# A two-layer diffusion step with linear attention: both passes of the linear attention re-ordered, its element-wise work spread differently over the engines

## The reference

```
z = h @ w_in                        # q, k (4 heads x 128), v, og (1024 each), r (2 x 16)
g = log_sigmoid(r @ gate_w + b)/16  # one decay per head, key column and direction
per chunk:  b = cumsum(g)
  o = (q*exp(b)) @ S + (sum over j<=i of q_i exp(b_i-b_j) k_j) v_j
  S = exp(b_last) * S + (k*exp(b_last-b))^T @ v
o = forward scan + backward scan
o = rms_norm per head(o, norm_g) * silu(og);   mix = o @ w_out
```

## Time and profile before

| | us |
|---|---|
| median of 3 runs | 2907.3 (2906.81 to 2907.7) |
| the profiled execution | 2904.5 |
| its span in the trace | 2902.7 |
| PE busy | 2770.3 (95%) |
| DVE busy | 1490.0 (51%) |
| ACT busy | 1267.4 (44%) |
| POOL busy | 159.4 (5%) |
| mean granted PE clock | 0.986 |

### The profile page before, as it was taken

The page is one execution under the profiler, slowest core; times in us unless marked ns, Lnnn a source line. Parts: engine busy times, 40 slices in busy tenths (PEclk is TensorE's granted clock), DMA queues, the critical chain, the costliest instruction groups (busy, mean ns, idle before and its releaser), DMA issues. The chain is left out here.

```text
span 2902.7 us, 39699 instructions
## 1 busy us (share of the span) xinstructions
PE 2770.3 (95%) x15219; PEld 2442.7 (84%) x15219; DVE 1490.0 (51%) x2282; ACT 1267.4 (44%) x2059; POOL 159.4 (5%) x260
## 2 busy tenths in 40 slices
PE   5999999999999999999999987778999999999998
PEld 3878887789999999999898876766899999999997
DVE  4255666655555445444413668775645554445444
ACT  5134445544444434333324765554543443334333
POOL 0000000000000000000000028810000000000000
PEclk9999999999999999999999998899999999999999
DMA  7643323533444444344214430024344344444443
GB/s 266 212 135 108 97 85 111 162 119 122 124 125 151 121 126 150 121 128 124 76 55 146 145 107 8 1 88 166 117 124 124 121 147 129 124 124 151 124 128 109
DMA packets 301702, 355.53 MB, mean 122 GB/s; under 512 B 22230, under 2 KB 244892, under 8 KB 300540
## 3 DMA queue, kind: packets, MB, share of 16 engines
q1 hardware_dynamic: 293840, 333.36, 37.0%
q10 hardware_dynamic: 5708, 12.42, 1.2%
q0 software_dynamic: 2016, 7.86, 0.8%
HBM read 338.27 MB, written 15.34 MB: 122 GB/s over the span
## 5 line engine op out<-in xcount | busy, mean ns | idle before, releaser
L1300 DVE TENSOR_TENSOR p_lo<-p_raw,p_hi 128x1024 fp32r<-128x1024 f32 x507 | 619.9, 1224 | 659.2 <-ACT p_hi L773 658.6
L773 ACT ACTIVATE p_hi<-p_raw 128x1024 fp32r<-128x1024 f32 x507 | 533.3, 1053 | 528.4 <-DMA p_raw<-mlp_w 413.1
L2087 PE MATMUL ps<-hm_hi,p_hi 128*128 128x384 f32 x1536 | 515.5, 336 | 0.8 <-DVE p_lo L1300 0.8
L2087 PE MATMUL ps<-hm_hi,p_lo 128*128 128x384 f32 x1536 | 515.8, 336 | 0.0
L2087 PE MATMUL ps<-hm_lo,p_hi 128*128 128x384 f32 x1536 | 514.4, 335 | 0.0
L2011 PE MATMUL ps<-p_hi,hid_hi 128*128 128x512 f32 x1152 | 362.6, 396 | 3.3 <-DVE p_lo L1300 3.3
L2011 PE MATMUL ps<-p_lo,hid_hi 128*128 128x512 f32 x1152 | 357.3, 391 | 0.0
L2011 PE MATMUL ps<-p_hi,hid_lo 128*128 128x512 f32 x1152 | 356.5, 391 | 0.0
L981 ACT ACTIVATE relu<-ps 128x384 f32<-128x384 f32 x192 | 94.5, 492 | 540.8 <-PE ps L2087 540.8
L1530 DVE TENSOR_TENSOR sqr<-relu 128x384 f32<-128x384 f32 x192 | 107.1, 558 | 390.7 <-ACT relu L981 390.7
L2087 PEld LDWEIGHTS ps<-hm_hi,p_hi 128*128 128x128 f32 x1536 | 288.4, 188 | 9.7 <-DVE p_lo L1300 2.5
(11 more groups left out here) (234 smaller groups left out, 3706.6 us busy)
## 6 DMA issues: line engine op xcount, KB each, us to landing
p_raw<-mlp_w SPq DMA_DIRECT2D x384, 512.0 KB, 3.9
mod_p<-mod_w SPq DMA_DIRECT2D x80, 512.0 KB, 4.1
p_raw<-gla_w_in SPq DMA_DIRECT2D x56, 512.0 KB, 3.6
p_raw<-gla_w_out SPq DMA_DIRECT2D x24, 512.0 KB, 3.3
mod_w<-mod_w SPq DMA_DIRECT2D x8, 1024.0 KB, 18.9
p_raw<-ab_w_in SPq DMA_DIRECT2D x14, 512.0 KB, 5.2
p_raw<-ab_w_out SPq DMA_DIRECT2D x24, 256.0 KB, 4.2
p_raw<-ab_w_out SPq DMA_DIRECT2D x12, 512.0 KB, 3.5
```

The costliest lines, as they stand in the source:

```text
L773: nc.scalar.activation(p_hi[s][:, :, 0:width], p_raw[s][:, :, 0:width], ACT.Copy).then_inc(pan_hi, 1)
L1300: V.tensor_tensor(p_lo[s][:, :, 0:width], p_raw[s][:, :, 0:width], p_hi[s][:, :, 0:width].bitcast(F32), ALU.subtract).then_inc(pan_lo, 1)
L2087: mm = M.matmul(ps[:, b, 0:GN], w[s][:, c, :], x[:, c, :], start=(c == 0 and x is hi and w is p_hi), stop=(c == DC - 1 and w is p_lo))
```

## The change

Five groups of edits, none of which changes what is computed.

1. The eight `turn_chunk`s of the projection stand in pairs behind its parts 3, 4, 5 and 6, no longer together behind part 7.
2. The last two groups of eight panels change places: og of group 2 comes before v of group 2, so the projection ends on `v_take`. ACT loads the exponential's table ahead of that `v_take` with an operation on one column. The loads of the masks and of the backward state go from ACT's queue to SP's. The two small exponentials `dec` move to tile 0's level index 3. PE no longer waits for all accumulators before the pass, POOL starts when all but two panels are used.
3. First pass: POOL does two operations a level with 512 columns each (at level 1: two with 256) into one of three buffers `gap` in place of four `dd`; ACT reads its half of a gap and writes in another order. `kh` is multiplied after level index 2. `state_step` stands after all levels, ahead of `q1`; `o_take` after level index 6; `att_out` does one head each after level indices 2 to 5.
4. Second pass: `from_state`, `update` and the state step run by pairs of heads. The gate is done by POOL in two operations of 1024 columns (times og, then times the reciprocal root, in place) in place of DVE's four of 256. `turn_o`, `gated_hi` and `gated_lo` run one to two tiles later.
5. The last two tiles are turned inside the output projection, after its panels 0 and 1. SP loads panel 2 after the last update and the others after the last `from_state`.

The diff, cut to its core:

```diff
+        def turned_after(part):
+            return (2 * part - 6, 2 * part - 5) if 3 <= part < 7 else ()
+        def value_panels(q):
+            return (q // DC % 2 == 0) != (q >= 4 * DC)
...
         def pool_gla(pool):
             pool.wait_ge(g_sum, 2 * GH)
-            pool.wait_ge(acc_done[GT - 1], ACC_AFTER_GLA_IN)
+            pool.wait_ge(pan_used, SLOTS + FEEDS_TO_GLA - 2)
...
-                if kind == "f" and n > 1:
-                    nc.gpsimd.tensor_tensor(x[:, :, 0, :], f_ref.broadcast_to(f[:, :, 0, :].shape), f[:, :, 0, :], ALU.subtract)
-                    nc.gpsimd.tensor_tensor(x[:, :, 1, :], b[:, :, 1, :], b_ref.broadcast_to(b[:, :, 1, :].shape),
-                                            ALU.subtract).then_inc(d_ready, 1)
+                x = out[:, :, :].rearrange("p u (b n) -> p b u n", n=n)
+                if n > 1:
+                    f_ref, b_ref = (y.unsqueeze(3).broadcast_to(f.shape) for y in (f_ref, b_ref))
+                    nc.gpsimd.tensor_tensor(x[:, :, 0::2], f, f_ref, ALU.subtract)
+                    nc.gpsimd.tensor_tensor(x[:, :, 1::2], b_ref, b, ALU.subtract).then_inc(d_ready, 1)
...
             pool_gla(pool)
+            pool.wait_ge(ob_taken, TILES)
+            for tile in range(TILES):
+                if tile:
+                    pool.wait_ge(o_sum, tile)
+                pool.wait_ge(og_in[tile % 2], 16 * (tile // 2 + 1))
+                if tile >= 2:
+                    pool.wait_ge(ot_ready, tile - 1)
+                nc.gpsimd.tensor_tensor(oo[tile % 2][:], o_b[tile][:], og[tile % 2][:], ALU.mult).then_inc(o_gate, 1)
+                pool.wait_ge(o_gate, tile + 1)
+                pool.wait_ge(o_rcp, tile + 1)
+                x = oo[tile % 2][:].rearrange("p (h v) -> p h v", h=GH)
+                nc.gpsimd.tensor_tensor(x, x, rs4[:, tile, 1, :].unsqueeze(2).broadcast_to([P, GH, DV]), ALU.mult).then_inc(o_nrm, 1)
... ACT, first pass
-                    nc.scalar.activation(out, dd[r % 4][:], ACT.Exp, scale=s).then_inc(e_ready, 1)
+                    x = gap_of(r)[:, 0::3, :] if kind == "S" else gap_of(r)[:, 1:3, :]
+                    y = out.rearrange("p h (b s n) -> p s (h b) n", s=2, n=n)
+                    nc.scalar.activation(y, x.rearrange("p s (b n) -> p s b n", n=n), ACT.Exp,
+                                         scale=-s if kind == "S" else s).then_inc(e_ready, 1)
... ACT, second pass
             for tile in range(TILES):
+                if tile >= 2:
+                    gated_hi(tile - 2)
                 head_norm(tile)
                 if tile + 2 < TILES - 1:
                     turn_take_k((2, 7)[tile % 2])
-                if tile:
-                    gated_hi(tile - 1)
-                    if tile + 1 < TILES:
-                        load_og(tile + 1)
+                if tile and tile + 1 < TILES:
+                    load_og(tile + 1)
...
                 if tile >= TILES - 2:
                     panel_hi()
... DVE, second pass
             for tile in range(TILES):
+                if tile >= 3:
+                    gated_lo(tile - 3)
...
                 if tile < TILES - 1:
-                    state_step(0, tile)
-                gate_head(tile)
+                    forward_step(tile, 0)
                 if tile:
-                    gated_lo(tile - 1)
+                    dve.wait_ge(o_ready, 2 * tile)
+                    V.tensor_tensor(o_b[tile][:], psf[:, 3 * 512:5 * 512], o_b[tile][:], ALU.add).then_inc(o_sum, 1)
+                    root_inverse(tile - 1)
+                if tile < TILES - 1:
+                    forward_step(tile, 1)
                 if tile >= TILES - 2:
                     panel_lo()
-            gated_lo(TILES - 1)
+            gated_lo(TILES - 3)
+            root_inverse(TILES - 1)
... PE, second pass
             for tile in range(TILES):
-                if tile:
-                    from_state(tile)
-                if tile < TILES - 1:
-                    update(TILES - 1 + tile, tile)
+                for pair in range(2):
+                    if tile:
+                        from_state(tile, pair)
+                    if tile < TILES - 1:
+                        forward_update(tile, pair)
                 if tile + 2 < TILES - 1:
                     turn_k0(tile + 2)
-                if tile:
-                    turn_o(tile - 1)
-            turn_o(TILES - 1)
-            pe.wait_ge(st_ready, 2 * (TILES - 1))
+                if tile >= 2:
+                    turn_o(tile - 2)
+            pe.wait_ge(st_ready, TILES - 1 + 2 * (TILES - 1))
+            pe.wait_ge(o_sum, TILES - 1)
... PE, output projection, behind each panel (ACT and DVE: gated_hi and gated_lo ahead of the panel's split)
+                    if layer and p < 2:
+                        turn_o(TILES - 2 + p)
```

More of the change, by code:

```diff
@@ L639, in factor_order @@
                         out += closing(TURNS[a - 1])
+                    if level == 2 and tile != 1:
+                        out.append(("k1", tile, 0))
                 if tile:
@@ L650, in gap_order @@
             for kind, tile, level in factor_order():
[L651 to L654, removed]
+                if kind == "M":
+                    out.append(("g", tile, level))
                 elif kind in ("k0", "q1"):
@@ L661, in gap_user, with gap_of, plain @@
         def gap_user(kind, tile, level):
-            if kind in ("k0", "q1"):
-                return factor_at[(kind, tile, level)]
-            return factor_at[("S" if kind == "f" and LEVELS[level] > 1 else "M", tile, level)]
+            return factor_at[("M" if kind == "g" else kind, tile, level)]
+        def gap_of(r):
+            return gap[r % len(gap)]
+        def plain(x):
+            return x[:, 0:2, :].rearrange("p u (h n) -> p (u h) n", n=P)
         def halves(t, level):
@@ L1519, in out_stage @@
                         pre_scale(layer, 0, 0)
+                    if layer and p < 2:
+                        gated_lo(TILES - 2 + p)
                     for k in turned_with(p):
@@ L2216, in update, with forward_update @@
                 for h in range(GH):
+                    last = M.matmul(psf[:, 5 * 512 + DV * h:5 * 512 + DV * (h + 1)], khn[n % 2][:, h, :],
+                                    gv[:, tile, DV * h:DV * (h + 1)], start=True, stop=True)
+                last.then_inc(upd_ready, 1)
+            def forward_update(tile, pair):
+                n = TILES - 1 + tile
+                if pair == 0:
+                    pe.wait_ge(khn_ready, n + 1)
+                pe.wait_ge(st_ready, n if tile == 0 else TILES - 1 + 2 * (tile - 1) + pair + 1)
+                for h in range(2 * pair, 2 * pair + 2):
                     last = M.matmul(psf[:, 5 * 512 + DV * h:5 * 512 + DV * (h + 1)], khn[n % 2][:, h, :],
@@ L2267, in _ @@
                             pe.wait_ge(ob_taken, a)
+                        else:
+                            for t in range(GT):
+                                pe.wait_ge(acc_read[t], acc_uses[t])
                         turn_k(kh, 3)
@@ L2278, in turn_k0, with from_state @@
                 turn_k(gk[:, tile], (2, 7)[tile % 2])
-            def from_state(tile):
+            def from_state(tile, pair):
                 pe.wait_ge(xt_ready, factor_at[("q0", tile, 0)] + 1)
```

164 lines of the change are left out of this document (92 added, 72 removed).

## The result

The kernel after takes 2854.9 us (median of 4 runs, 2853.3 to 2855.9) beside 2907.5 for the kernel before on the same chip: ratio 0.982, 95% interval 0.981 to 0.984. The forecast was 2869 with a range of 2853 to 2887. The profiled execution took 2855.85, its span 2854.1, so the spans differ by 48.6 us where the sum had 38.6. Most of the 13.8 us by which it came in under the forecast lie in the first pass. PE went from 2770.3 to 2752.2 us busy, DVE from 1490.0 to 1474.2, ACT stayed, and POOL went up by 21.

The account below looks back on a forecast made before the run. PE, busy 95% of the span, was taken as the bound, so only its waits could give much. Terms summing to -38.6 us took the profiled 2904.5 to 2865.9; with 2.8 for the median, 2868.7, told as 2869, range 2853 to 2887.

Parts of the forecast that it names:

- Edit 1 and the og group: Projection: transposes between parts gain 5.2 us; an og group in place of a v group loses 0.4.
- The turn: From projection to first pass: first gram at 1724.8 in place of 1729.92, a gain of 5.1 us.
- Tile 0: First tile of the first pass: a gain of 0.3 us for `kh` no longer at its head.
- The first pass: Eight tiles at 18.0 us in place of 20.17, bounded by DVE's 16.2 us of work: gain 17.4 us.
- the half-way step from 17.3 to the low-clock 18.6: First pass: a walked tile takes 17.3 us at full clock, 18.6 at low clock; 18.0 was taken.
- The second pass: First to last `from_state`: PE sets 4.9 and 4.45 us a tile, 1.6 for the start, 35.0 in all; gain 11.0.
- The tail: Last `from_state` to output panel 2: waits for ACT's and DVE's splits bind, 22.1 us against 22.3, gain 0.2.
- The offset: Whole kernel: the median of the runs lies 2.8 us above the profiled execution, added to the forecast.
- A: First pass keeps its pace, 20 us a tile, as several waits bind in turn: 2885 us; chance 0.15.
- B: Second pass becomes POOL's: 3.0 us per 1024-column operation, the gate sets 6.2 a tile: 2878 us; chance 0.08.
- C: First pass: POOL's four-index operation costs 2.1 us, not 1.1, a tile 28.6: slower, 2964 us; chance 0.05.
- D: The tail's waits don't bind and the low clock doesn't come: 2855 us; chance 0.10.

Follow-up runs that it names:

- Kernel 6: The kernel before with only the eight transposes moved, in pairs behind parts 3 to 6 of the projection: 2901.5 us.
- kernel 7: The kernel after with v before og at the projection's end, as before the change: 5.93 us from last panel to first gram of a level, 3.02 in the kernel after.
- Kernel 1: The kernel after with the multiplication of `kh` at the head of the tile again: 2857.2 us.
- kernels 5: The kernel after with the second pass's gate back on DVE, in four operations of 256 columns: 2862.8 us.
- 11: The kernel after with ACT's splits of output panels 0 and 1 in second-pass tiles 1 and 2, DVE's low parts left in 7 and 8: 2853.0 us.
- kernel 12: The kernel after with ACT's splits of output panels 0 and 1 in second-pass tiles 1 and 2, DVE's low parts in 2 and 8: 2849.15 us.
- kernel 2: The kernel after with the state step and `o_take` after level index 5 and heads in pairs after level indices 2 and 3: 2875.96 us.
- kernel 8: The kernel after with only the heads in pairs, after level indices 2 and 3: 2862.5 us.
- kernel 9: The kernel after with the heads in pairs and the state step after level index 5: 2878.2 us.
- kernel 10: The kernel after with ACT's splits of output panels 0 and 1 in second-pass tiles 1 and 2, DVE's low parts in 2 and 3: 2849.85 us.

## Why the prediction was right, and where its sizes were off

The direction and the place of each large gain were right, and so was the mechanism in the main: DVE sets the first pass once PE's wait before the last gram is gone, and PE sets the second. The time lies 0.5% under the forecast, near the low end of the range, and part of that is luck: the full clock of the first pass, as is said below. By its steps:

- **Edit 1 and the og group.** -5.2 and +0.4 were forecast. Kernel 6 gives -5.6 for the first, kernel 7 0.4 for the second, and the three waits of 0.4 are there (1.2 in all).
- **The turn.** -5.1 forecast, -5.18 measured; the first level's gram came 3.02 us behind the last panel, forecast 3.1.
- **Tile 0.** Wrong sign, +1.0 for -0.3. I let `kh` leave the head of the tile and forgot that the head lies ahead of this interval and the new place inside it. Kernel 1 shows it: tile 0 is 1.2 us shorter with `kh` at the head. In the kernel after 0.65 us of DVE and ACT's wait of 1.0 for it lie inside tile 0, and 0.76 of that came back in the stage before.
- **The first pass** is the term that was mis-sized: 17.4 forecast, 26.1 measured. The walk of a tile gave 17.3 us at full clock, and the steady tiles take 17.28 to 17.31, with DVE the one that is waited for. What was wrong was the half-way step from 17.3 to the low-clock 18.6, worth 0.7 x 8 = 5.6 us. In the profiled execution PE's clock was granted at 1.00 from tile 1 on. That is partly luck: in kernels 5, 7, 11 and 12, with the same first pass and the same wait of 1.84 us, one to three of six windows of 20 us were at about 0.91. But the price of the low clock was too high as well: kernel 12's steady tiles with it took 17.48 and 17.52 us, 0.2 more and not 1.3. Over its eight tiles PE's busy time is 5.1 us longer and its idle time 3.3 us shorter: most of the slower matmuls went into waits that were there anyway. The other 3.1 are the first two intervals and the last (15.59, 16.64, 16.56), which I counted as whole ones. The walk had the wait behind `turn_k` at 1.0 us; it is 1.83. The prediction says that both long waits of a tile are gone by the order. Only one is: the wait before the last gram. The other is as long as before, and the tile came out at 17.3 nevertheless because it was DVE's queue that filled the tile.
- **Which edit made the first pass faster** the prediction left open, and my theory of kernel 2 got it wrong. Kernels 8 and 9 show it: the step's place 16 us (with the heads in pairs), the heads' 7, `kh`'s 3 (of which up to 1.7 can be scatter), POOL's operations 3.7 when added to the kernel before and 1.7, no more than scatter, when taken from the kernel after. These don't add up to 26, since each was tried in one combination only.
- **The second pass.** 33.0 for 35.0: the spacing, 4.77 to 4.92 and 4.56 at the end, was forecast (4.9 and 4.45), but the 1.6 us for the start were not lost; the first interval is 4.19.
- **The tail.** 21.7 for 22.1, and its order is the forecast one: panel 0 at 8.7 (8.2), turn_o(7) at 15.9 (15.1). Versions 10 to 12 show that the named waits bind: without them it is 7.8 us shorter.
- **The offset.** The 2.8 us between the profiled execution and the median belonged to that execution; the kernel after's median lies 0.9 below its profiled one. These 3.7 us and the 10.0 in the stages make the 13.8 between 2868.7 and 2854.9.

The rivals: A fell (no tile over 17.31). B fell: POOL's pair takes 2.38 + 1.90 = 4.3 us, under PE's 4.9. The estimate by the Trainium skill (GPSIMD Engine Reference, "Elementwise — side-by-side cycle accounting") was 2.2 for either; the trace has 2.38 for the product of two full operands and 1.90 for the one in place with a broadcast operand. The port named there cost the tail nothing: its two `panel_lo` took 1.23 us each, with no POOL operation beside them. C fell: the four-index operation costs 1.06. Of D one half came true, the full clock, and the other did not; so its 2855 was met another way: the full clock, short first and last tiles, and a second pass without its start.

## What to carry to other kernels

When two engines wait for each other by turns, look for the one long instruction that stands ahead of a factor for which a matmul waits, and put it behind the last factor: here 1.6 us of DVE in another place was worth 16 us over eight tiles (with the heads in pairs), while halving the number of another engine's operations was worth at most 4. Walk one tile with measured durations to find the engine that fills it; where one engine fills the tile, the walk's time held even though a wait in it was off by 0.8 us. Give the low clock a price from rows, and remember that slower matmuls use up waits that were there anyway. Count the first and last rounds of a loop by what they contain. Before an engine is put to wait inside its own order for a split that could have been made earlier, move the split to where its owner idles, but not beside an operation that shares a path with it.

## What the runs showed of the hardware

- PE's granted clock from 1740 to 1860 us was 1.00 in each of six windows of 20 us in the kernel after, where PE waited at most 1.84 us at a time. It was 0.91 in all six in kernel 8, where PE waited 2.50 us once a tile, 0.91 in five of six in kernel 1 (2.43), and 0.83 or 0.91 in kernel 9 (2.20 before the last gram). The line is not sharp: with the same wait of 1.84 us, kernel 10 had 1.00 throughout like the kernel after, kernels 5 and 11 had 0.91 in one window and kernel 12 in three. Behind the wait in kernel 8 16 grams took 3.43 us, while eight take 1.05 at full clock. A wait can thus cost more than its length: PE's total busy time fell by 18 us with no less work, 14.9 of them in the first pass.
- A DVE operation with both inputs in SBUF and a POOL operation (reading SBUF) excluded each other in version 10: DVE's 1.22 us became 2.84 when it began 0.13 us into a POOL operation of 1.90, and it ended 1.07 us behind that operation; POOL's next took 3.34 for 2.37. The Trainium skill (SBUF — State Buffer, "SBUF: two separate sides") has this as an exclusive lock held for the whole instruction; by that rule, the trace agrees. DVE's sums with one input in PSUM lay beside the gate and kept their 1.21 to 1.23 us.
- A POOL subtraction of 512 columns with a four-index address in input and output takes 1.063 us in the mean, nearly as much as the plain one (1.040 to 1.051), and ACT's exponential written to PSUM in short runs 0.601, as in the kernel before.
